# Two chunk loads of every expert joined into one 4 MB transfer, in a hybrid SSD/attention/MoE layer

## The chip, the cores and the metric

The kernel runs on one core of one Trainium2 chip. The metric is the device time of one execution in microseconds, the median of several runs. The core has TensorE (PE; its weight loads are shown apart as PEld), VectorE (DVE), ScalarE (ACT), GpSimd (POOL) and SyncE (SP), which here issues nearly all the transfers. 16 DMA engines move the data between HBM and SBUF.

## What is computed

One layer for 320 tokens (256 of a prompt, 64 of a sample): an SSD mixer and a band attention share one input projection and one output projection, and then comes a mixture of 32 experts, of which each token uses four. The change lies in the loads of the experts' weights.

```python
D_MODEL = 1024; N_EXPERTS = 32; TOP_K = 4; D_FF = 1024

xp = xp + merge_heads(y_ssm, o, att_norm_g[l], w_out[l])
xp = xp + moe_ffn(rms_norm(xp, norm_ffn_g[l]), w_router[l], b_router[l],
                  w_gate_up[l], b_gate_up[l], w_down[l], b_down[l])
...
def expert_block(args):
    xb, e = args
    gu = xb @ w_gate_up[e] + b_gate_up[e]          # (rows, 1024) @ (1024, 2048)
    gate = jnp.minimum(gu[:, :D_FF], SWIGLU_LIMIT)
    up = jnp.clip(gu[:, D_FF:], -SWIGLU_LIMIT, SWIGLU_LIMIT)
    act = (up + 1) * gate * jax.nn.sigmoid(gate * SWIGLU_ALPHA)
    return act @ w_down[e] + b_down[e]             # (rows, 1024) @ (1024, 1024)
```

All weights are float32. `w_gate_up[e]` has 8 MB and `w_down[e]` 4 MB, so 32 experts are 403 million bytes.

## The kernel before

**The ring.** `ring` is an SBUF tensor of six slots of 16 KB per partition, 2 MB each. The front of the kernel (input and output projection, attention, router) streams its weights through slots 0 to 4 (`FRONT_SLOTS`). After it, an expert's weights take all six slots, as six chunks: chunks 0 to 3 are quarters of `w_gate_up[e]` (`GU_CHUNKS`), chunks 4 and 5 halves of `w_down[e]` (`DN_CHUNKS`). `EXPERT_SLOT = (1, 2, 3, 4, 0, 5)` says which slot a chunk takes; slots 1 and 2 of chunks 0 and 1 are neighbours. The ring holds one expert and no more, so a chunk of the next expert is loaded as soon as PE has made its last use of the same chunk of this one.

**The rows.** Partition p of half h of an expert's matrix holds four successive rows of `w_gate_up[e]`, 32 KB in a piece. Chunk 0 takes the first two of the four for h = 0, chunk 1 the other two; chunks 2 and 3 do the same for h = 1. Chunk 3 is loaded as two transfers of 1 MB (L335, L336), of which the second counts on the semaphore `half_full`. All other chunks are one transfer of 2 MB with rows of 16 KB (L294, the helper `load`).

**SP, the queue of the loads.** SP issues in program order. Before the experts it loads chunk 0 of expert 0 once the last use of slot 1 in the front is over, chunk 1 once that of slot 2 is over (`wait_used`), then waits for three semaphores and issues four transfers of the attention's relative bias (L349, semaphore `bias_in`), and then the other chunks of expert 0. The loop `Fori(1, NE)` at L354 then loads expert n of the order: for each chunk it waits until the chunk is used (`used`: `gs_used` for chunk 0, `gs_used1` for chunk 1, `gs_used2`, `gu_mm`, `ds_used`, `d_mm`) and issues.

**PE, the user.** Tokens of an expert are worked on in blocks of up to 64 (`CAP`). `expert_pass(b, n)` is one block: for each gate/up chunk a wait for its slot's semaphore `w_full` and 16 matmuls (two 8-matmul rows of k), with `gather(b + 1)` before chunk 2; then `combine(b - 1)`, turning and placing; then chunks 4 and 5 at L2040, with `bias_products(b + 1)` between them. Most experts have one block. Four have two in this data (36 blocks in all); the weights stay in the ring for the second, and the semaphores of the first block are waited for by nobody, since SP waits for the count `first`, that of the expert's last block.

**DVE in the front.** DVE waits for `bias_in` at L1005 before it masks a corner of the bias (L1006), and after that it does `add_ssd(1)`, an addition of a part of the output projection (L979). PE waits for that addition (`out_ev`) before its first attention scores (L1695).

Of the kernel before, what the change touches and what calls it, by code (L numbers as in the profile page):

```python
# [34 lines left out]
FRONT_SLOTS = 5  # L35
# [7 lines left out]
N_IN, N_OUT = len(W_IN_CHUNKS), 3  # L43
FRONT = N_IN + N_OUT
GU_CHUNKS, DN_CHUNKS = 4, 2
EXPERT_SLOT = (1, 2, 3, 4, 0, 5)
# [13 lines left out]
def build(nc, x_prompt, x_sample, cache_k, cache_v, state_conv, state_ssm,  # L60
# [11 lines left out]
    with ctx:  # L72
        def sb(name, shape, dt=f32):
            return ctx.enter_context(nc.sbuf_tensor(name, shape, dt))

        def sem(name):
            return ctx.enter_context(nc.semaphore(name))


        ring = sb("ring", [128, SLOTS, SLOT])  # L80
# [185 lines left out]
        s = {n: sem(n) for n in names}  # L266
# [3 lines left out]
        w_full = [sem(f"w_full{i}") for i in range(SLOTS)]  # L270
# [8 lines left out]
        def slot_of(chunk):  # L279
            return chunk % FRONT_SLOTS  # L280
# [5 lines left out]
        def expert_arrival(c):  # L286

            return 16 * (len(range(EXPERT_SLOT[c], FRONT, FRONT_SLOTS)) if EXPERT_SLOT[c] < FRONT_SLOTS else 0) + 16


        @block.sync
        def _(sp):
            def load(slot, k, src):
                sp.dma_start(ring[:, slot, :].rearrange("p (k n) -> p k n", k=k), src).then_inc(w_full[slot], 16)  # L294

            def wait_used(i):

                if i < 3:
                    sp.wait_ge(s["proj_mm"], 4 * i + 4)
                elif i < 5:  # L300
                    sp.wait_ge(s["proj_mm"], 12 + NT * (i - 2))
                elif i < N_IN:
                    sp.wait_ge(s["lane_mm"], (LANE_Q, LANE_K, LANE_V)[i - 5])
                elif i < N_IN + 2:
                    sp.wait_ge(s["out_mm"], SSD_PARTS)
                else:
                    sp.wait_ge(s["out_mm"], OUT_PARTS)

            for t in range(2):
                sp.dma_start(x[:, t, :], x_prompt[0, 128 * t:128 * t + 128, :]).then_inc(x_in[t], 16)  # L310
            sp.dma_start(x[0:SS, 2, :], x_sample[0, :, :]).then_inc(x_in[2], 16)
            w3 = w_in[0].rearrange("(k p) n -> p k n", p=128)
            for i, c in enumerate(W_IN_CHUNKS):
                if i >= FRONT_SLOTS:
                    wait_used(i - FRONT_SLOTS)
                if i == 0:
                    slot = ring[:, 0, :].rearrange("p (k n) -> p k n", k=KD)
                    sp.dma_start(slot[:, 0:4, :], w3[:, 0:4, c:c + 512]).then_inc(half_full, 16)
                    sp.dma_start(slot[:, 4:8, :], w3[:, 4:8, c:c + 512]).then_inc(w_full[0], 16)
                else:  # L320
                    load(slot_of(i), KD, w3[:, :, c:c + 512])
            wo = w_out[0].rearrange("(k p) n -> p k n", p=128)
            for j in range(N_OUT):
                wait_used(N_IN + j - FRONT_SLOTS)
                load(slot_of(N_IN + j), 4, wo[:, 4 * j:4 * j + 4, :])

            def load_expert(e, c):
                if c < GU_CHUNKS:
                    w, h, k0, k = w_gate_up[0], c // 2, 2 * (c % 2), 2
                else:  # L330
                    w, h, k0, k = w_down[0], c - GU_CHUNKS, 0, 4
                rows = w[bass.ds(e, 1)].rearrange("a (h p k) n -> p (a h) k n", h=2, p=128)
                if c == GU_CHUNKS - 1:
                    slot = ring[:, EXPERT_SLOT[c], :].rearrange("p (k n) -> p k n", k=k)
                    sp.dma_start(slot[:, 0:1, :], rows[:, h, k0:k0 + 1, :]).then_inc(w_full[EXPERT_SLOT[c]], 16)  # L335
                    sp.dma_start(slot[:, 1:2, :], rows[:, h, k0 + 1:k0 + 2, :]).then_inc(half_full, 16)  # L336
                else:
                    load(EXPERT_SLOT[c], k, rows[:, h, k0:k0 + k, :])

            for c in range(GU_CHUNKS + DN_CHUNKS):  # L340
                slot = EXPERT_SLOT[c]
                wait_used(max(range(slot, FRONT, FRONT_SLOTS)) if slot < FRONT_SLOTS else N_IN)
                load_expert(0, c)
                if c == 1:
                    sp.wait_ge(s["ext_out"], 17)
                    sp.wait_ge(s["seg_mm"], 6)
                    sp.wait_ge(s["y_mm"], 5)
                    for q in range(4):
                        sp.dma_start(bias[:, 2 * q:2 * q + 2, :], bass.AP(  # L349
                            table_d, head_of(q // 2, 2 * (q % 2)) * 383, [[1, 128], [2 * 383, 2], [1, 256]]))\  # L350
                            .then_inc(s["bias_in"], 16)
            sp.wait_ge(s["order_ready"], 1)
            used = ["gs_used", "gs_used1", "gs_used2", "gu_mm", "ds_used", "d_mm"]
            with sp.Fori(1, NE) as n:  # L354
                e = sp.value_load(order[0:1, bass.ds(n, 1)], min_val=0, max_val=NE - 1)
                first = sp.value_load(before[0:1, bass.ds(n, 1)], min_val=1, max_val=MAX_BLOCKS)
                for c in range(GU_CHUNKS + DN_CHUNKS):

                    sp.wait_ge(s[used[c]], first)
                    load_expert(e, c)  # L360

            for t in range(2):
                sp.wait_ge(s["fin_ready"], t + 1)
                sp.dma_start(y_prompt[0, 128 * t:128 * t + 128, :], xn[:, t, :]).then_inc(s["y_out"], 16)
            sp.wait_ge(s["fin_ready"], 3)
            sp.dma_start(y_sample[0, :, 0:HALF], xn[0:SS, 2, 0:HALF]).then_inc(s["y_out"], 16)
            sp.wait_ge(s["y_out"], 4 * 16)
            sp.wait_ge(s["vt_out"], NT * 16)
            sp.wait_ge(s["kt_out"], NT * 16)
            sp.wait_ge(s["cso_out"], 2 * 16)  # L370
            sp.wait_ge(s["sout_out"], 2 * 16)
# [999 lines left out]
        def _(pe):  # L1371
# [31 lines left out]
            n = [0]  # L1403
# [79 lines left out]
            for t in range(NT):  # L1483
                rows = ROWS[t]
# [32 lines left out]
            for t in range(NT):  # L1517
                rows, hc = ROWS[t], slice(HCOL[t], HCOL[t] + ROWS[t])
# [458 lines left out]
            def expert_pass(b, n, beside=None):  # L1977

                pe.wait_ge(s["xt_ev"], b + 1)
                for c in range(GU_CHUNKS):  # L1980
# [3 lines left out]
                        places(0)  # L1984
                    if not beside and c == 2:
                        gather(b + 1)
                    pe.wait_ge(w_full[EXPERT_SLOT[c]], expert_arrival(c) + 16 * n)
                    w = ring[:, EXPERT_SLOT[c], :].rearrange("p (k n) -> p k n", k=2)

                    def gate_up(kk, m):  # L1990
# [60 lines left out]
            turn(0)  # L2051
            idle_products(7, 2)
            expert_pass(0, 0, beside=True)
            pe.wait_ge(s["zeros_ready"], 1)
            total = pe.value_load(blocks[0:1, 0:1], min_val=NE, max_val=MAX_BLOCKS)
# [5 lines left out]
def head_of(group, n):  # L2061

    return 4 * group + 2 * (n % 2) + n // 2
# [89 lines left out]
```

## Time and profile before

| | |
|---|---|
| median of 3 runs | 1272.1 us |
| lowest, highest | 1271.05, 1275.47 us |
| profiled execution | 1272.46 us, with a span of 1270.7 us in the trace |
| PE busy | 1232.4 us, 97% of the span |
| DVE, ACT, POOL busy | 38%, 17%, 3% |
| DMA | 436.6 MB, 344 GB/s over the span |
| granted PE clock | 1.0 but for a few us |

The page cuts the span into 40 slices of 31.8 us. From the tenth slice on (286 us) the experts run. There PE is busy throughout, and the DMA engines move 427 to 429 GB/s in all slices but those in which an expert has its second block: 259, 333, 303 and 292 GB/s. So two resources are nearly full at once, and what counts is which of the two is waited for, and where.

Times in the text are from the start of the span. "Expert 0" is the first in the order, and an expert's start is the start of its first matmul at L1993.

### The profile page before, as it was taken

The page shows a single profiled execution, that of the slowest core. Times are in us where ns is not written, and L with a number is a line of the kernel's source. Part 1 is how long each engine was busy: PE and PEld are TensorE (multiplying, and loading weights), DVE is VectorE, ACT ScalarE, POOL GpSimd, SP SyncE. Part 2 cuts the span into 40 slices and gives each one's busy share as a digit, 9 for nine tenths or more (in the row PEclk, how much of TensorE's full clock was granted, in tenths as well). Part 3 has the DMA queues.
Part 4 walks back from the last instruction along what each step waited for, and adds up shares of the span by engine and source line. Part 5 has one row for each costly group of instructions (what it writes and reads, how often), then busy time and mean ns, then how long its engine had stood idle before and what let it go on. Part 6 is the DMA issues. An engine that isn't in the chain of part 4 may idle for free.

```text
span 1270.7 us, 17573 instructions
## 1 busy us (share of the span) xinstructions
PE 1232.4 (97%) x6386; PEld 553.0 (44%) x6387; DVE 480.8 (38%) x1038; ACT 215.2 (17%) x444; POOL 39.0 (3%) x67
## 2 busy tenths in 40 slices
PE   9999999999999999999999999989999999999996
PEld 7656754653334443434333434333434333334332
DVE  3743545466532332324322224222234232234234
ACT  1032223562201111011001111010111110111102
POOL 2000002401000000000000000000000000000000
PEclk9999999999999999999999999999999999999999
DMA  9631234328999969999998999997999999799995
GB/s 329 219 133 68 83 132 137 130 109 341 428 428 427 427 259 429 429 428 426 428 386 333 429 427 429 427 427 303 417 427 427 428 429 426 292 429 428 427 427 239
DMA packets 48202, 436.60 MB, mean 344 GB/s; under 512 B 6293, under 2 KB 7437, under 8 KB 19510
## 3 DMA queue, kind: packets, MB, share of 16 engines
q1 hardware_dynamic: 44000, 429.28, 81.2%
q0 software_dynamic: 2176, 6.74, 1.6%
q10 hardware_dynamic: 2006, 0.31, 0.2%
q8 instruction: 13, 0.21, 0.1%
q14 instruction: 7, 0.06, 0.0%
HBM read 432.59 MB, written 3.72 MB: 343 GB/s over the span
## 4 chain that ended last, share of the span: by engine, by line
PE 83%; DMA 13%; DVE 2%; issue 1%; ACT 0%; DVEq 0%; SPq 0%; ACTq 0%
PE PS L1993 33%; PE PS L2040 17%; DMA ring<-in_w_gate_up_dram 12%; PE PS L1422 6%; PE PS L1431 5%; PE PS L1886 4%; PE PS L1376 4%; PE PS L1917 3%; PE PS L1911 2%; PE PS L1433 1%; PE PS L1465 1%; PE PS L1755 1%; PE PS L1974 1%; PE PS L1729 1%; PE PS L1613 1%
## 5 line engine op out<-in xcount | busy, mean ns | idle before, releaser
L1993 PE MATMUL PS<-ring,r 128*64 128x512 f32 x2304 | 510.7, 593 | 16.1 <-DMA ring<-in_w_gate_up_dram 15.7
L1993 PEld LDWEIGHTS PS<-ring,r 128*64 128x64 f32 x2304 | 167.5, 137 | 331.8 <-issue 289.2
L2040 PE MATMUL PS<-ring,r 128*64 128x512 f32 x1152 | 261.5, 595 | 4.5 <-ACT r L778 0.5
L1318 DVE TENSOR_SCALAR r<-PS 128x256 f32<-128x256 f32 x72 | 27.2, 419 | 333.2 <-PE PS L1993 333.1
L2040 PEld LDWEIGHTS PS<-ring,r 128*64 128x64 f32 x1152 | 81.8, 137 | 135.6 <-issue 129.0
L1222 DVE SCALAR_TENSOR_TENSOR r<-PS,gprev,r 128x512 f32<-128x512 f32 x185 | 127.9, 743 | 0.6 <-PE PS L1917 0.6
L1346 DVE TENSOR_TENSOR yy<-PS,yy 128x512 fp32r<-128x512 f32 x36 | 24.9, 691 | 193.4 <-ACT yy L783 193.4
L1376 PE MATMUL PS<-ident,r 128*128 128x128 f32 (+4 forms) x491 | 70.3, 282 | 1.7 <-DMA r<-in_x_sample_dram 0.5
L1422 PE MATMUL PS<-r,ring 128*128 128x323 f32 x256 | 71.9, 436 | 0.0
L767 ACT ACTIVATE r<-PS 128x512 f32<-128x512 f32 x35 | 20.9, 597 | 295.4 <-PE PS L1886 295.4
L783 ACT ACTIVATE yy<-PS 128x512 fp32r<-128x512 f32 x36 | 21.5, 597 | 276.8 <-PE PS L2040 276.8
L1376 PEld LDWEIGHTS PS<-ident,r 128*128 128x128 f32 (+4 forms) x491 | 58.2, 181 | 20.9 <-DVE r L1328 8.9
L1422 PEld LDWEIGHTS PS<-r,ring 128*128 128x128 f32 x256 | 48.1, 189 | 22.5 <-issue 1.9
L771 ACT ACTIVATE r<-r 128x256 f32<-128x256 f32 x72 | 26.9, 416 | 183.3 <-DVE r L1318 183.3
L1886 PE MATMUL PS<-r,pm 128*64 128x512 bf16 x420 | 51.4, 379 | 1.4 <-DVE pm L1195 1.4
L1917 PE MATMUL PS<-yy,place 64*128 64x512 f32 x296 | 44.5, 418 | 0.8 <-ACT yy L783 0.8
L1431 PE MATMUL PS<-ring,r 128*128 128x512 f32 x96 | 42.1, 593 | 0.0
L1886 PEld LDWEIGHTS PS<-r,pm 128*64 128x64 bf16 x420 | 25.2, 110 | 35.7 <-issue 20.1
L1917 PEld LDWEIGHTS PS<-yy,place 64*128 64x128 f32 x296 | 24.9, 184 | 34.4 <-issue 30.8
L1190 DVE COPY pcur<-pg 128x3 f32 x36 | 6.1, 169 | 79.2 <-issue 79.2
L774 ACT ACTIVATE place<-PS 128x384 fp32r<-128x384 f32 x36 | 17.7, 492 | 82.4 <-PE PS L1911 82.4
L1431 PE MATMUL PS<-ring 128*128 128x512 f32 x64 | 29.4, 603 | 2.2 <-DVE r L979 2.2
(349 smaller groups left out, 864.0 us busy)
## 6 DMA issues: line engine op xcount, KB each, us to landing
ring<-in_w_gate_up_dram SPq DMA_DIRECT2D x96, 2048.0 KB, 15.6
ring<-in_w_down_dram SPq DMA_DIRECT2D x64, 2048.0 KB, 16.2
ring<-in_w_gate_up_dram SPq DMA_DIRECT2D x64, 1024.0 KB, 16.2
ring<-in_w_in_dram SPq DMA_DIRECT2D x7, 2048.0 KB, 15.6
ring<-in_w_out_dram SPq DMA_DIRECT2D x3, 2048.0 KB, 7.5
ring<-in_w_in_dram SPq DMA_DIRECT2D x2, 1024.0 KB, 9.0
r<-in_x_prompt_dram SPq DMA_DIRECT2D x2, 512.0 KB, 4.1
r<-in_x_prompt_dram POOLq DMA_DIRECT2D x2, 512.0 KB, 4.8
```

Source lines behind the costliest of these rows:

```text
L771: a.activation(sg[:, part], ug[:, part], ACT.Sigmoid, scale=ALPHA).then_inc(s["sig_ready"], 1)
L1222: v.scalar_tensor_tensor(xx, bank(banks[i]), gprev[:, t:t + 1], xx, ALU.mult, ALU.add).then_inc(s["o_ev"], 1)
L1318: v.tensor_scalar(ug[:, part], bank(0)[:, part], LIMIT, None, ALU.min).then_inc(s["g_ready"], 1)
L1346: v.tensor_tensor(yy2[:, 1, :], bank(2), yy2[:, 0, :].bitcast(f32), ALU.subtract)\
L1376: return nc.tensor.transpose(out, in_, ident[0:k, 0:k])
L1422: last = mm(PS[:, b, 0:HC], w[:, k, 128 * m:128 * m + 128], hT[:, k, :], start=(k == 0), stop=(k == KD - 1))
L1431: return mm(PS[:, b, :], lhs, rhs, start=first, stop=end)
L1886: last = mm(PS[64 * h:64 * h + 64, 3, :], pm[:, t, 64 * h:64 * h + 64], xb[t][:, part, 512 * h:512 * h + 512], start=(t == 0 and part == 0 ...
L1911: last = mm(bank(banks[4]), place[:, 256:384], yy2[:, part, :], start=(part == 0), stop=(part == 1))
L1917: last = mm(bank(banks[2 * t + h]), place[half, 128 * t:128 * t + 128], yy2[half, part, :], start=(part == 0), stop=(part == 1))
L1993: last = mm(PS[64 * h:64 * h + 64, m, :], xt[:, k % 4, k // 4, :], w[:, kk, D * m + 512 * h:D * m + 512 * h + 512], start=False, stop=(k = ...
L2040: last = mm(PS[64 * h:64 * h + 64, 2, :], at[:, kk, c, :], w[:, kk, 512 * h:512 * h + 512], start=(c == 0 and kk == 0), stop=(c == 1 and k ...
```

## The change

Chunks 0 and 1 become one transfer of 4 MB, from rows of 32 KB to the 32 KB of slots 1 and 2 in each partition. It counts on the semaphore of slot 1. In the loop SP issues it after `gs_used1`, the last use of chunk 1; `gs_used` isn't waited for any more. PE waits for it before chunk 0, and no more before chunk 1. For expert 0 the transfer is issued once slot 1 and slot 2 are both free.

```diff
                 rows = w[bass.ds(e, 1)].rearrange("a (h p k) n -> p (a h) k n", h=2, p=128)
-                if c == GU_CHUNKS - 1:
+                if c == 0:
+                    pair = ring[:, EXPERT_SLOT[0]:EXPERT_SLOT[0] + 2, :].rearrange("p s (k n) -> p (s k) n", k=k)
+                    sp.dma_start(pair, rows[:, h, 0:4, :]).then_inc(w_full[EXPERT_SLOT[0]], 16)
+                elif c == GU_CHUNKS - 1:
...
             for c in range(GU_CHUNKS + DN_CHUNKS):
-                slot = EXPERT_SLOT[c]
-                wait_used(max(range(slot, FRONT, FRONT_SLOTS)) if slot < FRONT_SLOTS else N_IN)
+                if c == 1:
+                    continue
+                for slot in EXPERT_SLOT[0:2] if c == 0 else EXPERT_SLOT[c:c + 1]:
+                    wait_used(max(range(slot, FRONT, FRONT_SLOTS)) if slot < FRONT_SLOTS else N_IN)
                 load_expert(0, c)
-                if c == 1:
+                if c == 0:
                     sp.wait_ge(s["ext_out"], 17)
...
-            used = ["gs_used", "gs_used1", "gs_used2", "gu_mm", "ds_used", "d_mm"]
+            used = ["gs_used1", None, "gs_used2", "gu_mm", "ds_used", "d_mm"]
...
-                for c in range(GU_CHUNKS + DN_CHUNKS):
+                for c in (0, 2, 3, 4, 5):
...
-                    pe.wait_ge(w_full[EXPERT_SLOT[c]], expert_arrival(c) + 16 * n)
+                    if c != 1:
+                        pe.wait_ge(w_full[EXPERT_SLOT[c]], expert_arrival(c) + 16 * n)
```

SP's queue before the experts: the last load of the output projection, the first chunks of expert 0, the bias (`r<-bias_table_clipped`) and chunk 2. Before:

```order
L294 DMA ring<-in_w_out_dram 128x4x1024 [waits lane_mm]
L294 DMA ring<-in_w_gate_up_dram 128x4096 [waits lane_mm] x2
L349 DMA r<-bias_table_clipped 128x2x256 [waits y_mm,seg_mm,ext_out]
L349 DMA r<-bias_table_clipped 128x2x256 x3
L294 DMA ring<-in_w_gate_up_dram 128x4096 [waits out_mm]
```

and changed:

```order
L294 DMA ring<-in_w_out_dram 128x4x1024 [waits lane_mm]
L335 DMA ring<-in_w_gate_up_dram 128x8192 [waits lane_mm]
L354 DMA r<-bias_table_clipped 128x2x256 [waits y_mm,seg_mm,ext_out]
L354 DMA r<-bias_table_clipped 128x2x256 x3
L294 DMA ring<-in_w_gate_up_dram 128x4096 [waits out_mm]
```

Chunk 0 no longer goes out ahead of chunk 1 at its own wait; both stand right before the bias.

SP's queue in the loop over experts, one pass. Before:

```order
L294 ISA [waits gs_used]
L294 DMA ring<-in_w_gate_up_dram 128x4096
L294 ISA [waits gs_used1]
L294 DMA ring<-in_w_gate_up_dram 128x4096
L294 ISA [waits gs_used2]
L294 DMA ring<-in_w_gate_up_dram 128x4096
```

and changed:

```order
L335 ISA [waits gs_used1]
L335 DMA ring<-in_w_gate_up_dram 128x8192
L294 ISA [waits gs_used2]
L294 DMA ring<-in_w_gate_up_dram 128x4096
L338 ISA [waits gu_mm]
L338 DMA ring<-in_w_gate_up_dram 128x2048
```

What stood behind `gs_used` now stands behind `gs_used1`; all the rest keeps its place.

PE at the first block, chunks 0 and 1 of expert 0 (in the loop the same waits stand against a register). Before:

```order
L1993 MATMUL PS<-ring,r 64x512 [waits w_full1,xt_ev]
L1993 MATMUL PS<-ring,r 64x512
L1966 MATMUL PS<-spare,ones 128x66 [waits turns_ready]
L1993 MATMUL PS<-ring,r 64x512 x6
L1993 MATMUL PS<-ring,r 64x512 [waits w_full2]
L1993 MATMUL PS<-ring,r 64x512 x7
```

and changed:

```order
L1999 MATMUL PS<-ring,r 64x512 [waits w_full1,xt_ev]
L1999 MATMUL PS<-ring,r 64x512
L1971 MATMUL PS<-spare,ones 128x66 [waits turns_ready]
L1999 MATMUL PS<-ring,r 64x512 x14
L1381 MATMUL PS<-ident,bej 1x128 [waits bej_ready]
```

The wait for slot 2 in the middle is gone; the one for slot 1 now stands for both.

## Rows read from the trace of the kernel before

**Rows 1.** The page: PE's busy time, and the gate/up matmuls (idle before, by releaser)

```profile
PE 1232.4 (97%) x6386; PEld 553.0 (44%) x6387; DVE 480.8 (38%) x1038; ACT 215.2 (17%) x444; POOL 39.0 (3%) x67
...
L1993 PE MATMUL PS<-ring,r 128*64 128x512 f32 x2304 | 510.7, 593 | 16.1 <-DMA ring<-in_w_gate_up_dram 15.7
```

**Rows 2.** Busy time by stretch: engines, granted clock, DMA share, GB/s

```profile
504.70:609.70 105.00, 104.54 (x556) 41.78 (x552) 34.63 (x76) 12.13 (x24) 0.00 (x0) 1.00 1.01 428
611.30:640.70 29.40, 26.69 (x138) 9.96 (x138) 8.68 (x20) 3.03 (x6) 0.00 (x0) 1.00 1.01 428
```

**Rows 3.** PE's timeline (start, duration, idle before): blocks' first matmuls, and waits

```profile
426.54 7.04 PE L1993 MATMUL PS<-ring,r 128*64 128x512 f32 x32
...
452.72 7.04 PE L1993 MATMUL PS<-ring,r 128*64 128x512 f32 x32
...
611.26 3.65 PE L1993 MATMUL PS<-ring,r 128*64 128x512 f32 x16 [1.17 <-DMA ring<-in_w_gate_up_dram]
616.15 3.65 PE L1993 MATMUL PS<-ring,r 128*64 128x512 f32 x16 [1.24 <-DMA ring<-in_w_gate_up_dram]
...
640.73 3.65 PE L1993 MATMUL PS<-ring,r 128*64 128x512 f32 x16 [1.17 <-DMA ring<-in_w_gate_up_dram]
...
655.49 2.80 PE L1993 MATMUL PS<-ring,r 128*64 128x512 f32 x12 [0.20 <-DMA ring<-in_w_gate_up_dram]
668.83 7.04 PE L1993 MATMUL PS<-ring,r 128*64 128x512 f32 x32
...
885.00 7.04 PE L1993 MATMUL PS<-ring,r 128*64 128x512 f32 x32
...
1101.08 7.04 PE L1993 MATMUL PS<-ring,r 128*64 128x512 f32 x32
...
1231.97 7.04 PE L1993 MATMUL PS<-ring,r 128*64 128x512 f32 x32
```

**Rows 4.** SP's timeline (start, duration): issues of chunks 0 and 1

```profile
327.49 0.33 SPq L294 DMA_DIRECT2D ring<-in_w_gate_up_dram  x1
...
456.51 0.34 SPq L294 DMA_DIRECT2D ring<-in_w_gate_up_dram  x1
...
459.94 0.33 SPq L294 DMA_DIRECT2D ring<-in_w_gate_up_dram  x1
...
1108.30 0.33 SPq L294 DMA_DIRECT2D ring<-in_w_gate_up_dram  x1
```

**Rows 5.** Timelines of SP, DVE and PE (in this order) around the bias

```profile
183.99 0.34 SPq L294 DMA_DIRECT2D ring<-in_w_gate_up_dram  x1
...
188.77 2.59 SPq L349 DMA_DIRECT2D r<-bias_table_clipped  x4
...
198.39 0.48 DVE L1006 MEMSET r<- 64x512 f32 x1 [4.37 <-DMA r<-bias_table_clipped]
198.91 0.75 DVE L979 SCALAR_TENSOR_TENSOR r<-PS,stat,r 128x512 f32<-128x512 f32 x1
...
201.07 0.68 DVE L1012 TENSOR_TENSOR r<-r,PS 64x512 f32<-64x512 f32 x1 [0.82 <-PE PS L1616]
...
211.21 0.75 DVE L979 SCALAR_TENSOR_TENSOR r<-PS,stat,r 128x512 f32<-128x512 f32 x1 [3.73 <-PE PS L1431]
...
200.80 0.71 PE L1695 MATMUL PS<-r 64*128 64x128 f32 x8
...
207.47 3.70 PE L1431 MATMUL PS<-ring 128*128 128x512 f32 x8 [0.79 <-DVE r L979]
```

**Rows 6.** Busy time by stretch, while chunk 3 of an expert is transferred

```profile
650.10:655.00 4.90, 4.90 (x30) 1.67 (x24) 0.00 (x0) 0.60 (x1) 0.00 (x0) 1.00 1.04 433
```

**Rows 7.** The chain: the same eight matmuls, twice

```profile
251.08 3.65 PE PS L1755 x8
...
258.28 5.29 PE PS L1755 x8
```

**Rows 8.** Busy time by stretch: the granted clock (0.54) in the second of these

```profile
258.00:260.00 2.00, 2.00 (x5) 0.98 (x5) 1.33 (x4) 1.99 (x8) 0.00 (x0) 0.54 0.00 0
```

## The prediction

> **What bounds the kernel now.** First the page. PE is busy 97% of the span, and the gate/up matmuls waited only 15.7 us for their weights [rows 1], so PE looks like the bound. Then the busy time by stretch: while experts with one block follow each other, the DMA engines are full too, at 428 GB/s [rows 2]. So the third view decides, PE's timeline. A block of an expert whose weights are there takes PE 26.18 us, from 426.54 to 452.72 [rows 3]. An expert's 12.58 million bytes need more: where PE waits for them, the period is 640.73 - 611.26 = 29.47 us [rows 3], which is 427 GB/s, or **4.912 us for each 2 MB chunk**. PE gains 3.29 us per expert on the transfers. What lets it run at its own pace in between is a cushion. While an expert has its second block, nothing is loaded until the ring is released, and afterwards the next expert lies there well before it is wanted. Every single expert then eats 3.29 us of that lead. Second blocks begin at 452.72, 668.83, 885.00 and 1101.08, eight blocks apart, which at PE's own pace would be 209.4 us and is 216.1 to 216.2: three stretches of 6.7 us lost each, in the two experts before every next second block (611.26 and 640.73 for the first stretch). Before 452.72 and after 1101.08 no block is late [rows 3]. The waits come in three small pieces, 1.17 and 1.24 us at chunks 0 and 1, 0.20 us within chunk 3 [rows 3]. So what bounds the kernel is PE for most of the experts, and the transfers for the last two of each stretch; how many these are is set by the cushion. What a change of the loads does to the time is what it does to the cushion.
>
> **The cushion after the change.** I call the expert whose second block starts at 452.72 expert 5, the next ones 6 to 12; expert 12 is the next with two blocks (starts 640.73 and 668.83). Two things shorten the lead. The pair is issued at the last use of chunk 1 instead of chunk 0: 459.94 instead of 456.51, 3.43 us later [rows 4]. And PE may start an expert only when 4 MB of it have landed, where before it could start with 2 MB and was held last by chunk 3. The sum for this stretch: before, the second half of chunk 3 of expert 12 let PE go on at 655.49 [rows 3]. It was chunk-length 40 of those issued from 456.51 on (six experts of 6, and 4), 40 x 4.912 = 196.47, which leaves 2.51 us of fixed delay. The changed order issues from 459.94 on, and expert 12 can start after 38 chunk-lengths (six experts of 6, and the pair): 459.94 + 186.65 + 2.51 = 649.1. Its first block then takes 26.18 us unhindered (chunk 2 lands 4.9 us after the start and is wanted after 8.6; the rest has as much slack), and its second block starts at 675.3 instead of 668.83: **6.4 us later**. Three such stretches (the periods 216.17 and 216.08 say they are alike) make **19.3 us**.
>
> The same rule makes the two outer parts late, which weren't. Up to expert 5: the pair of expert 2 is issued at 327.49, where chunk 1 was [rows 4]; the pair of expert 5 is there after three experts of 6 and 2, 20 chunk-lengths: 327.49 + 98.24 + 2.51 = 428.2 against a start at 426.54 [rows 3]: **1.7 us**. After the last second block: pair issue at 1108.30 [rows 4], the pair of the last expert is there after 26 chunk-lengths, 1108.30 + 127.71 + 2.51 = 1238.5, against 1231.97 [rows 3]: **6.5 us**. Together 1.7 + 19.3 + 6.5 = **27.5 us**. None of it can be won back, since each stretch starts anew from a full ring. That the queue doesn't run dry, which would cost more: the pair of expert 7 is issued when expert 6 has used its chunk 1, by PE's pace at 452.72 + 26.18 + 7.2 = 486.1, while the transfers of expert 6 last till 459.94 + about 2 + 29.5 = 491.4. Later in the stretch, the pair is ready to go some 12 us ahead.
>
> **The front.** One more place comes before the experts. SP issues chunk 1 of expert 0 at 183.99 and the bias at 188.77, in that order on one queue [rows 5]. Chunk 0 had gone long before. Now the pair of 4 MB is issued at 183.99, and the bias stands behind 2 MB more: 4.9 us. DVE already waited 4.37 us for the bias, until 198.39, and so did the addition at 198.91 to 199.66 behind it [rows 5]; PE needs that addition for its scores at 200.80 [rows 5], so there is a slack of 1.1 us. Moved by 4.9 us, the addition ends at 204.6 and PE's scores start 3.8 us late. Behind them DVE has only an idle 0.82 us to give (before 201.07), so its chain is 4.1 us late, and PE's L1431 at 207.47 waits for that chain [rows 5]. From there on DVE waits for PE (3.73 us before 211.21), so PE leads and the delay stays: **4.1 us**. The nearest bounds: other queues' traffic shares the engines at that time and would share the pair instead of the bias, so 3.5 to 5.3 us for the bias, 2.5 to 4.5 us for the end. I take the 4.1 of the plain chunk length.
>
> **What is removed.** PE's wait before chunk 1 and one transfer per expert; SP is idle nearly all the time and its issue of 0.33 us hides. That leaves the rate of longer rows. The only rows of another length in the experts are the 8 KB of chunk 3, which moved at 433 GB/s in one stretch [rows 6], no slower than 16 KB at 428 [rows 2]; so length isn't what holds the rate. I take no gain. If the pairs alone went at 433 (4.84 us per chunk-length), 8, 3 x 14 and 10 of them on the three kinds of stretches save 0.07 us each, 4.2 us.
>
> The Trainium skill (DMA: Bandwidth & Descriptors, "Anatomy of one DMA" and "Rules for kernel authors") gives one transfer about 2 us fixed plus its bytes at 436 GB/s, and advises to join small transfers into a large one. By that, an expert's seven queued transfers would take 14 us beyond their bytes, and one fewer would save 2 us each time; the 29.47 us for 12.58 million bytes [rows 3] leave room for at most 0.6 us in all, so the trace doesn't agree for transfers that are queued. The 2.51 us above, paid once per stretch, is the place of that fixed part.
>
> **The sum.** 1272.46 us of the profiled execution (0.4 us above the median, and 1.8 above its own span) + 27.5 + 4.1 = 1304.1 us.
>
> **The rivals.**
> - *The clock falls.* Now all of an expert's waiting stands in one piece of up to 3.3 us (29.47 - 26.18), at four experts of each long stretch and two of the last. In the trace of before, eight matmuls that take 3.65 us took 5.29 at a granted clock of 0.54, half speed (1.2 of 2.4 GHz), after a stretch of small matmuls [rows 7, 8]: 1.64 us. Against it: with the waits in pieces of 1.24 us at most, the clock held. Where an expert waits after it anyway, the loss is hidden; it counts at the last expert of a stretch and in the front, five places: up to 8.2 us, 1312. One or two of them lie within my range. The Trainium skill (TensorE: Matmul & The Clock Gate, "HAM oscillation") describes waits for weights after which each tile starts at the slow clock; no stretch of this trace shows a wait as long as the one expected here.
> - *The front absorbs the bias.* If POOL's traffic moves out of the bias's way and gives back most of the 4.9 us, 1300.
> - *Long rows stream a little faster*: by the 4.2 us above, 1300.
> - *The wait only moves.* If the lead were long enough for both demands, only the front would be left: 1276.6. Against it stands that PE runs out of data at 611 already before the change [rows 3].
> - *Faster than before.* 32 KB rows would have to lift the transfers so far that the lead outlives a stretch. Expert 12's second block keeps its 668.83 if the 14 chunk-lengths in pairs take 62.3 instead of 68.8 us, 471 GB/s; that is the point from which it decides. At 500 GB/s a pair takes 8.4 us, each of the three stretches ends 3.6 us early, the outer parts even: 1272.5 - 10.8 + 2.7 = 1264. No stretch of the trace moves more than 433 [rows 6].
>
> **How the numbers follow.** The forecast, with no or one or two falls of the clock, 0.74; the clock falling nearly everywhere 0.08; the front absorbed 0.06; rows faster by a little 0.06; only the front 0.02; faster than before 0.03; the rest 0.01. The predicted time is 1304. The range takes in both milder cases and half of the clock's: 1298 to 1310. A measurement of this kernel can tell about 0.3% (3.8 us) from no change. Slower 0.95, same 0.02, faster 0.03.
>
> **What the profile would show.** The gate/up matmuls' wait for their weights up from 15.7 to about 45 us, nearly all before chunk 0 and in pieces of about 3.3 us, in experts 9 to 12, 16 to 19, 23 to 26 and the last two, with 1 to 2 us at expert 5; distances between second blocks of 222.6 us instead of 216.1; the pair landing as one; still 427 GB/s in full stretches; DVE's wait for the bias at 9 us instead of 4.37 and a gap in PE of about 4 us at 201; PE's busy time unchanged but for the clock. Wrong would be: distances still at 216 (the lead suffices), or below (faster rows), or above 225 (a queue run dry, a slow clock), and no gap in the front.

## The result, and the profile after

The changed kernel takes 1310.07 us (median of 3 runs, 1309.82 to 1310.24) against 1272.1 us: 1.0296 of the time before, 95% interval 1.0282 to 1.0310. That is 38 us slower, on the side and by the mechanism forecast, 6 us above the 1304 and at the very edge of the range of 1298 to 1310. The profiled execution took 1309.82 us with a span of 1308.1 us, 37.4 us more than the span before. Two disturbed executions are left out of the ratios and medians below: one of the sixth kernel's four (3259 us) and one of the kernel before beside it (1816 us).

The page of the changed kernel, in the order of its parts: busy time, the slices' transfer rate, the queues, and the groups of the gate/up matmuls.

```profile
PE 1246.0 (95%) x6386; PEld 555.8 (42%) x6387; DVE 481.9 (37%) x1038; ACT 215.3 (16%) x444; POOL 39.1 (3%) x67
...
GB/s 328 204 129 66 81 135 126 106 139 302 428 431 426 405 197 430 429 430 428 432 348 291 429 428 435 424 430 257 383 434 428 424 428 426 217 433 422 427 427 207
DMA packets 43595, 436.60 MB, mean 334 GB/s; under 512 B 5782, under 2 KB 6926, under 8 KB 18999
...
L1999 PE MATMUL PS<-ring,r 128*64 128x512 f32 x2304 | 521.5, 606 | 33.5 <-DMA ring<-in_w_gate_up_dram 33.1
```

PE's wait for the gate/up weights rose from 15.7 us [rows 1] to 33.1 us, and the same 2304 matmuls are busy 10.8 us longer. The forecast was a wait of 45 us in pieces of 3.3; part of that lateness shows as slow matmuls instead, and 33.1 + 10.8 = 43.9 us is near it. The rate of a full slice is about what it was (424 to 435 GB/s). The mean fell from 344 to 334 GB/s because the pauses of the transfers, at the second blocks, grew. The packets tell that the 4 MB transfer really goes out as rows of 32 KB: 4607 fewer than before.

PE's timeline of the changed kernel, from expert 0 to the second block of expert 12, as start, duration and idle time before (expert 5 starts at 438.67, its second block at 466.59, expert 12 at 662.33, its second block at 688.56):

```profile
296.58 1.08 PE L1999 MATMUL PS<-ring,r 128*64 128x512 f32 x4 [0.41 <-DVE r L1218]
...
409.28 7.09 PE L1999 MATMUL PS<-ring,r 128*64 128x512 f32 x32 [1.40 <-DMA ring<-in_w_gate_up_dram]
...
438.67 8.78 PE L1999 MATMUL PS<-ring,r 128*64 128x512 f32 x32 [2.98 <-DMA ring<-in_w_gate_up_dram]
...
466.59 7.04 PE L1999 MATMUL PS<-ring,r 128*64 128x512 f32 x32
...
574.20 8.78 PE L1999 MATMUL PS<-ring,r 128*64 128x512 f32 x32 [2.69 <-DMA ring<-in_w_gate_up_dram]
...
603.58 7.09 PE L1999 MATMUL PS<-ring,r 128*64 128x512 f32 x32 [1.27 <-DMA ring<-in_w_gate_up_dram]
...
632.95 8.78 PE L1999 MATMUL PS<-ring,r 128*64 128x512 f32 x32 [2.97 <-DMA ring<-in_w_gate_up_dram]
...
662.33 7.09 PE L1999 MATMUL PS<-ring,r 128*64 128x512 f32 x32 [1.29 <-DMA ring<-in_w_gate_up_dram]
...
688.56 7.04 PE L1999 MATMUL PS<-ring,r 128*64 128x512 f32 x32
...
910.46 7.04 PE L1999 MATMUL PS<-ring,r 128*64 128x512 f32 x32
...
1132.47 7.04 PE L1999 MATMUL PS<-ring,r 128*64 128x512 f32 x32
...
1269.47 7.09 PE L1999 MATMUL PS<-ring,r 128*64 128x512 f32 x32 [1.27 <-DMA ring<-in_w_gate_up_dram]
```

Where before each late expert waited in three pieces [rows 3], all waiting stands before chunk 0. It begins at expert 9 in this stretch, where before it began at expert 11. The distances between second blocks, which answer to [rows 3], are 221.97, 221.90 and 222.01 us instead of 216.1 to 216.2. The two kinds of rows also differ: after a wait of 2.7 us or more the 32 matmuls take 8.78 us, after 1.3 us they take 7.09. The busy time by stretch tells why; the column before the last two is the granted clock:

```profile
574.20:577.60 3.40, 3.40 (x12) 1.21 (x14) 0.85 (x4) 0.00 (x0) 0.00 (x0) 0.70 1.05 448
603.60:607.00 3.40, 3.40 (x16) 1.18 (x18) 0.92 (x5) 0.00 (x0) 0.00 (x0) 1.00 1.04 443
633.00:636.40 3.40, 3.40 (x10) 1.02 (x12) 0.85 (x4) 0.00 (x0) 0.00 (x0) 0.58 1.03 439
```

And the front, which answers to [rows 5]: SP's, DVE's and PE's timelines.

```profile
184.26 0.34 SPq L335 DMA_DIRECT2D ring<-in_w_gate_up_dram  x1
188.96 2.10 SPq L354 DMA_DIRECT2D r<-bias_table_clipped  x4
...
206.39 0.48 DVE L1011 MEMSET r<- 64x512 f32 x1 [12.16 <-DMA r<-bias_table_clipped]
206.91 0.75 DVE L984 SCALAR_TENSOR_TENSOR r<-PS,stat,r 128x512 f32<-128x512 f32 x1
...
207.81 1.23 PE L1700 MATMUL PS<-r 64*128 64x128 f32 x8 [6.63 <-DVE r L984]
208.97 6.05 PE L1436 MATMUL PS<-ring 128*128 128x512 f32 x8
...
216.47 3.70 PE L1436 MATMUL PS<-ring 128*128 128x512 f32 x8
```

DVE waits 12.16 us for the bias instead of 4.37, PE has a gap of 6.63 us, and right behind it eight matmuls take 6.05 us that take 3.70 later; the mean granted clock from 208.9 to 215.0 us was 0.60.

The 37.4 us of the span, by place:

| place | forecast | before | after | measured |
|---|---|---|---|---|
| start to expert 0 | +4.1 | 289.25 | 296.58 | +7.3 |
| expert 0 to second block of expert 5 | +1.7 | 163.47 | 170.01 | +6.5 |
| three distances between second blocks | +19.3 | 648.36 | 665.88 | +17.5 |
| fourth second block to last expert | +6.5 | 130.89 | 137.00 | +6.1 |
| last expert to the end | 0 | 38.73 | 38.63 | -0.1 |

(289.25 is the first matmul of expert 0 before the change, by its PE timeline.)

### The profile page after: what moved, and what is told of

It reads as the page before. It is cut to its first block, busy times and chain, and to the rows that moved or that the text cites. A ratio compares the mean times of both kernels' runs of the same rounds, so it can differ in the third digit from the quotient of the medians.

```text
span 1308.1 us, 17480 instructions
## 1 busy us (share of the span) xinstructions
PE 1246.0 (95%) x6386; PEld 555.8 (42%) x6387; DVE 481.9 (37%) x1038; ACT 215.3 (16%) x444; POOL 39.1 (3%) x67
## 2 busy tenths in 40 slices
DMA packets 43595, 436.60 MB, mean 334 GB/s; under 512 B 5782, under 2 KB 6926, under 8 KB 18999
## 4 chain that ended last, share of the span: by engine, by line
PE 69%; DMA 26%; DVE 2%; issue 2%; ACT 0%; DVEq 0%; SPq 0%; ACTq 0%
PE PS L1999 30%; DMA ring<-in_w_gate_up_dram 26%; PE PS L2046 11%; PE PS L1427 5%; PE PS L1436 5%; PE PS L1381 3%; PE PS L1891 3%; PE PS L1922 2%; PE PS L1438 1%; PE PS L1470 1%; PE PS L1760 1%; PE PS L1916 1%; PE PS L1734 1%; PE PS L1979 1%; PE PS L1618 1%
## 5 line engine op out<-in xcount | busy, mean ns | idle before, releaser
L1999 PE MATMUL PS<-ring,r 128*64 128x512 f32 x2304 | 521.5, 606 | 33.5 <-DMA ring<-in_w_gate_up_dram 33.1
L2046 PE MATMUL PS<-ring,r 128*64 128x512 f32 x1152 | 261.5, 595 | 4.5 <-ACT r L783 0.5
L1351 DVE TENSOR_TENSOR yy<-PS,yy 128x512 fp32r<-128x512 f32 x36 | 24.9, 692 | 193.4 <-ACT yy L788 193.4
## 6 DMA issues: line engine op xcount, KB each, us to landing
ring<-in_w_down_dram SPq DMA_DIRECT2D x64, 2048.0 KB, 19.3
```

The costliest lines, as they stand in the source:

```text
L1351: v.tensor_tensor(yy2[:, 1, :], bank(2), yy2[:, 0, :].bitcast(f32), ALU.subtract)\
L1999: last = mm(PS[64 * h:64 * h + 64, m, :], xt[:, k % 4, k // 4, :], w[:, kk, D * m + 512 * h:D * m + 512 * h + 512], start=False, stop=(k = ...
L2046: last = mm(PS[64 * h:64 * h + 64, 2, :], at[:, kk, c, :], w[:, kk, 512 * h:512 * h + 512], start=(c == 0 and kk == 0), stop=(c == 1 and k ...
```

## The experiments

The theory is the forecast's: an expert's weights are wanted with a lead that the ring gives after each second block; the change takes 3.4 us of it by issuing later and about 3 by starting later; and the bias behind 4 MB instead of 2 is a separate loss in the front. The rivals: only one of the two halves matters; the long transfer itself costs or gains; the front's loss has another cause. All times of the kernel before beside these runs lie between 1271.7 and 1272.4 us in the median.

**One half each.** The first kernel only issues later:

```diff
-            used = ["gs_used", "gs_used1", "gs_used2", "gu_mm", "ds_used", "d_mm"]
+            used = ["gs_used1", "gs_used1", "gs_used2", "gu_mm", "ds_used", "d_mm"]
```

> Two transfers as before; only in the loop SP issues chunk 0 after the last use of chunk 1 (3.43 us later), PE's waits and the front stay. Cushion theory: each stretch between second blocks loads 3.4 us later, so the three long stretches and the last each lose 3.4, the first about 0.6: 1272.1 + 14 = 1286 (1284 to 1289), distances between second blocks 219.5 us. Rival, that the later issue hides behind the queue and only PE's later start costs: 1272, distances of 216.1.

Measured: 1286.9 us (1286.04 to 1288.3) against 1272.4, ratio 1.011 (1.0094 to 1.0127). PE's timeline, first matmuls of three of the second blocks (the durations are cut at the edge of the stretch asked for) and the last expert before the second of them:

```profile
455.66 1.89 PE L1993 MATMUL PS<-ring,r 128*64 128x512 f32 x8
...
646.83 3.65 PE L1993 MATMUL PS<-ring,r 128*64 128x512 f32 x16 [1.15 <-DMA ring<-in_w_gate_up_dram]
651.73 3.65 PE L1993 MATMUL PS<-ring,r 128*64 128x512 f32 x16 [1.25 <-DMA ring<-in_w_gate_up_dram]
...
661.59 2.79 PE L1993 MATMUL PS<-ring,r 128*64 128x512 f32 x12 [0.19 <-DMA ring<-in_w_gate_up_dram]
...
674.94 5.33 PE L1993 MATMUL PS<-ring,r 128*64 128x512 f32 x24
...
894.36 6.18 PE L1993 MATMUL PS<-ring,r 128*64 128x512 f32 x28
```

The first two distances are 219.3 and 219.4 us, 3.3 above those before. The rival (nothing lost) is out. The waits stay in three small pieces, and no matmul behind them is slow. The total fits the forecast partly by luck: from expert 0 to the second block of expert 5 it is 2.4 us more than before (0.6 was forecast), from the fourth second block to the last expert 1.4 more (3.4 was forecast).

The second kernel only starts later, PE waiting for both chunks:

```diff
+                    if c == 0:
+                        pe.wait_ge(w_full[EXPERT_SLOT[1]], expert_arrival(1) + 16 * n)
                     pe.wait_ge(w_full[EXPERT_SLOT[c]], expert_arrival(c) + 16 * n)
```

> Two transfers issued as before; only PE waits for chunk 1 as well before it starts chunk 0. Cushion theory: what held PE before was the second half of chunk 3, which let an expert start when about 1.4 chunk-lengths had landed; now it is 2, some 3 us more in each of the three long stretches and the last, nothing in the first: 1272.1 + 12 = 1284 (1282 to 1287), distances of 219 us, waits of 3.3 us in one piece before chunk 0. Rival, that only the issue matters: 1272.

Measured: 1291.64 us (1287.53 to 1293.1), ratio 1.0145 (1.0121 to 1.0168). Both halves cost, then, but this one more than forecast. The profiled execution has distances of 220.9, 219.3 and 221.0 us. The last expert before the next second block, in the first and the second of these:

```profile
648.31 8.68 PE L1995 MATMUL PS<-ring,r 128*64 128x512 f32 x32 [3.04 <-DMA ring<-in_w_gate_up_dram]
...
869.21 7.09 PE L1995 MATMUL PS<-ring,r 128*64 128x512 f32 x32 [1.59 <-DMA ring<-in_w_gate_up_dram]
```

Where that expert's matmuls run at full clock the distance is the 219 forecast; where they run slow it is 1.6 us more. So 3.2 us of the 7.6 over the forecast are the clock. Another 1.7 are in the part up to the second block of expert 5, forecast at nothing: expert 5 already waits 1.5 us. The rest is spread: the slow-free distance is 3.2 and not 3 us longer, from the fourth second block to the last expert it takes 134.3 us (1116.42 to 1250.68) instead of 130.9, where 3 were forecast, and this execution reached expert 0 at 290.06 us instead of 289.25.

**Both halves, as two transfers and as one.** The third kernel has both edits above and still moves 2 MB at a time in rows of 16 KB. The fourth has the change itself, but only in the loop:

```diff
-                if c == GU_CHUNKS - 1:
+                if c == 0 and joined:
+                    pair = ring[:, EXPERT_SLOT[0]:EXPERT_SLOT[0] + 2, :].rearrange("p s (k n) -> p (s k) n", k=k)
+                    sp.dma_start(pair, rows[:, h, 0:4, :]).then_inc(w_full[EXPERT_SLOT[0]], 16)
+                elif c == GU_CHUNKS - 1:
...
-            used = ["gs_used", "gs_used1", "gs_used2", "gu_mm", "ds_used", "d_mm"]
+            used = ["gs_used1", None, "gs_used2", "gu_mm", "ds_used", "d_mm"]
...
-                for c in range(GU_CHUNKS + DN_CHUNKS):
+                for c in (0, 2, 3, 4, 5):
                     sp.wait_ge(s[used[c]], first)
-                    load_expert(e, c)
+                    load_expert(e, c, joined=True)
...
-                    pe.wait_ge(w_full[EXPERT_SLOT[c]], expert_arrival(c) + 16 * n)
+                    if c != 1 or beside:
+                        pe.wait_ge(w_full[EXPERT_SLOT[c]], expert_arrival(c) + 16 * n)
```

> Both at once in the loop, still as two transfers of 2 MB with rows of 16 KB, front as before. Cushion theory: the whole loss of the loop without the front, and without any gain of long rows: 1272.1 + 31 to 34 = 1303 to 1306 (distances 222 to 223 us, the clock's fall at some waits included). Rival, that the transfer of 4 MB itself (its length, its rows) costs: clearly below the loop-only kernel of this call.

> The 4 MB transfer in the loop alone; expert 0 is loaded as before (chunk 0 early, chunk 1 ahead of the bias). The changed kernel's trace puts 7.3 us of its loss before the experts and 30.1 after: 1310.1 - 7.3 = 1302.8 (1301 to 1304), with no gap of PE near 201 us. If 32 KB rows save 0.1 us per pair, it is up to 3 us below the kernel with two transfers; if they do nothing, equal. Rival, that the late bias isn't the cause of the front's loss: 1310.

Measured: 1302.87 us (1302.11 to 1303.35) with two transfers, ratio 1.0237 (1.0220 to 1.0254), and 1302.35 us (1301.12 to 1306.77) with one, ratio 1.0241 (1.0217 to 1.0265). They can't be told apart. So the size of the transfer and the length of its rows are worth nothing that shows in the time; the loss in the loop is that of the two waits. In the timelines a small gain is there. Starts of two late experts in a row, first of the kernel with two transfers, then with one:

```profile
593.63 7.09 PE L1995 MATMUL PS<-ring,r 128*64 128x512 f32 x32 [1.34 <-DMA ring<-in_w_gate_up_dram]
623.09 8.68 PE L1995 MATMUL PS<-ring,r 128*64 128x512 f32 x32 [3.05 <-DMA ring<-in_w_gate_up_dram]
```

```profile
595.21 8.59 PE L1996 MATMUL PS<-ring,r 128*64 128x512 f32 x32 [2.98 <-DMA ring<-in_w_gate_up_dram]
624.58 7.09 PE L1996 MATMUL PS<-ring,r 128*64 128x512 f32 x32 [1.47 <-DMA ring<-in_w_gate_up_dram]
```

29.46 us per expert against 29.37: 0.09 us for each joined pair. Over all late experts in a row the means are 29.45 (10 periods) and 29.38 us (11 periods), 0.07 us apart. Whether the longer rows give that or the one transfer fewer was not separated.

**The front alone.** The fifth kernel has the 4 MB transfer for expert 0 only, the sixth holds chunk 0 of expert 0 back to the time of chunk 1 and sends both as two transfers of 2 MB. The edit of the sixth:

```diff
             for c in range(GU_CHUNKS + DN_CHUNKS):
-                slot = EXPERT_SLOT[c]
-                wait_used(max(range(slot, FRONT, FRONT_SLOTS)) if slot < FRONT_SLOTS else N_IN)
+                for slot in EXPERT_SLOT[0:2] if c < 2 else EXPERT_SLOT[c:c + 1]:
+                    wait_used(max(range(slot, FRONT, FRONT_SLOTS)) if slot < FRONT_SLOTS else N_IN)
                 load_expert(0, c)
```

> The 4 MB transfer for expert 0 alone; the loop over the other experts as before. If the front's loss stands by itself: DVE's wait for the bias near 12 us instead of 4.4, a gap of PE of about 6.6 us after 201 us with the clock at half behind it, the first expert 7.3 us later, 1272.4 + 7.5 = 1280 (1278.5 to 1281.5). Rival, that the 7 us are partly taken back in the experts' cushion: 1275 or less.

> Only the front: chunk 0 of expert 0 is held back to the time of chunk 1, and both go as two transfers of 2 MB with rows of 16 KB right behind each other, ahead of the bias. If the bias is late by the bytes ahead of it and by the other queue's loads that now fall on it: as with the one transfer, 1280, DVE's wait for the bias 11.5 to 12.5 us. Rival, that packets of 32 KB hold the other queue's packets of 4 KB back and so push them onto the bias: DVE's wait 9 to 10.5 us, 1276 to 1278.

Measured: 1280.99 us (1280.65 to 1281.02), ratio 1.0073 (1.0055 to 1.0091), and 1281.86 us (1279.79 to 1282.31), ratio 1.0074 (1.0053 to 1.0096). DVE's wait for the bias, of the one and of the other:

```profile
206.17 0.48 DVE L1011 MEMSET r<- 64x512 f32 x1 [12.21 <-DMA r<-bias_table_clipped]
```

```profile
209.12 0.48 DVE L1006 MEMSET r<- 64x512 f32 x1 [12.20 <-DMA r<-bias_table_clipped]
```

The wait is the same to 0.01 us (the sixth kernel's front as a whole ran 3 us later in this execution), so rows of 32 KB aren't what holds the bias back. Bytes are. The transfers of the kernel before from 184 to 198 us, when the bias was in, and of the changed one from 184 to 206 us (q1 is SP's queue, q0 GpSimd's; packets and MB):

```profile
q1 hardware_dynamic: 1232, 3.15, 70.5%
q0 software_dynamic: 321, 1.05, 24.3%
```

```profile
q1 hardware_dynamic: 1232, 5.24, 64.5%
q0 software_dynamic: 640, 2.10, 25.6%
```

The pair's 4.2 MB keep the engines longer, and GpSimd's transfers are held up with the bias and then move beside it. The trace's packets tell the two apart. Before, the last packet of chunk 1 ended at 191.46 us, and the bias's own packets (1024 of 1 KB) ran from 192.43 to 197.95, with 0.46 MB of GpSimd's within that time. In the changed kernel the pair ended at 197.30, and the bias ran from 196.93 to 205.89, with 1.79 MB of GpSimd's within it. So of the 8.0 us by which the bias came later (206.39 against 198.39) 4.5 are the later start, near the 4.9 forecast, and 3.4 the slower transfer of the bias itself, 8.96 us instead of 5.52.

The seventh kernel is the changed one with the bias issued ahead of expert 0's pair, the eighth the one before with the bias ahead of chunk 1. For both the edit is one of place: the call `load_expert(0, c)` stands behind the block that waits for `ext_out`, `seg_mm` and `y_mm` and issues the bias, not ahead of it.

> The changed kernel, with the bias issued ahead of expert 0's pair. If the front's loss is the order on SP's queue: no gap of PE at 201 us, DVE's wait for the bias under 4 us, 1310.1 - 7.7 = 1302.4 (1301 to 1304.5). Rival, that the pair now comes late for expert 0 or delays later loads of the front: 1305 or more. Rival, that the bias isn't the cause: 1310.

> The kernel before, with the bias issued ahead of chunk 1 of expert 0 instead of behind it. DVE's wait of 4.4 us should shrink to under 1.5 us, and yet the time stay, since the chain behind the bias is released by PE's matmuls at 201 us as well: 1272.4 (1271 to 1273.5). Rival, that the wait for the bias is on the path: 1270 or less.

Measured: 1300.19 us (1299.28 to 1302.38), ratio 1.0227 (1.0208 to 1.0245), and 1272.13 us (1270.71 to 1273.61) against 1271.97, ratio 1.0004 (0.9994 to 1.0013). The seventh takes away 9.9 us of the change's 38, somewhat more than the 7.7 forecast, and PE has no gap:

```profile
198.04 0.48 DVE L1011 MEMSET r<- 64x512 f32 x1 [3.63 <-DMA r<-bias_table_clipped]
...
201.19 0.71 PE L1700 MATMUL PS<-r 64*128 64x128 f32 x8
```

That order is therefore the cause of the front's loss. One expectation failed: DVE's wait didn't go under 1.5 us in the kernel before. With the bias ahead of chunk 1 it is 3.91 us there, 3.63 in the changed kernel. The bias is then issued at 188.8 us, after the three semaphores, and its packets still run from 190.66 to 197.50, hardly earlier than the 197.95 of the kernel before. GpSimd's transfers and the load behind the bias move in the same time; what each of them costs it wasn't tried. In the kernel before nothing is to be gained from the order, as expected: PE leads there.

**Why expert 5 is late.** The tenth kernel is the loop-only one, with GpSimd's three loads of the last norm's gain held back:

```diff
             pool.wait_ge(s["gates_held"], 1)
+            pool.wait_ge(s["d_mm"], 6)
```

> The loop-only kernel, with GpSimd's three loads of the last norm's gain (768 KB) held back until the sixth block's end, when the transfers pause. If these loads on expert 1's transfers are what made expert 5 late by 3 us more than the sum said: from the first matmul of expert 0 to the second block of expert 5 165 to 168.5 us instead of 170.5 (before: 163.5), 1302.4 - 3 = 1299.5 (1298 to 1301.5). Rival, that they don't matter: 170.5 us, 1302.4.

Measured: 1301.97 us (1299.46 to 1304.56), ratio 1.0230 (1.0212 to 1.0248); the total doesn't tell it from 1302.35 and missed the 1298 to 1301.5 expected. The timelines do. Expert 0, expert 5 and its second block, of the loop-only kernel and of this one:

```profile
287.83 1.08 PE L1996 MATMUL PS<-ring,r 128*64 128x512 f32 x4 [0.41 <-DVE r L1215]
...
430.35 8.78 PE L1996 MATMUL PS<-ring,r 128*64 128x512 f32 x32 [2.97 <-DMA ring<-in_w_gate_up_dram]
...
458.28 1.03 PE L1996 MATMUL PS<-ring,r 128*64 128x512 f32 x4
```

```profile
288.03 1.08 PE L1997 MATMUL PS<-ring,r 128*64 128x512 f32 x4 [0.41 <-DVE r L1216]
...
428.12 8.78 PE L1997 MATMUL PS<-ring,r 128*64 128x512 f32 x32 [2.60 <-DMA ring<-in_w_gate_up_dram]
...
456.05 7.04 PE L1997 MATMUL PS<-ring,r 128*64 128x512 f32 x32
```

Expert 5 starts 140.1 us after expert 0 instead of 142.5, and expert 4 has no wait any more. From expert 0 to the second block of expert 5 it is 168.0 us, within the expectation, where the loop-only kernel, the changed one and the seventh all have 170.0 to 170.5. So 2.4 us of this part's 6.5 are those loads, which fell on the transfers of expert 1. Further on this execution lost more than that to the clock: its expert 12 took 10.02 us for 32 matmuls and its expert 19 8.59, and the first two distances are 224.7 and 223.3 us instead of 221.9 and 221.8.

**The other way round.** If less lead costs, more should pay. The ninth kernel loads chunk 0 in two halves of 1 MB and issues the first half after 8 of its 16 matmuls (semaphores for the halves added, bias ahead of chunk 1 as in the eighth):

```diff
+                if c == 0 and halves is not None:
+                    slot = ring[:, EXPERT_SLOT[c], :].rearrange("p (k n) -> p k n", k=k)
+                    sp.dma_start(slot[:, 0:1, :], rows[:, h, k0:k0 + 1, :]).then_inc(s["gain_in"], 16)
+                    sp.wait_ge(s["gs_used"], halves * 2 + 1)
+                    sp.dma_start(slot[:, 1:2, :], rows[:, h, k0 + 1:k0 + 2, :]).then_inc(w_full[EXPERT_SLOT[c]], 16)
```

> The other way round: chunk 0 of every expert in two transfers of 1 MB, the first issued after 8 of the chunk's 16 matmuls, bias ahead of expert 0's chunk 1, all else as before. Cushion theory: after a second block the transfers start 1.7 us earlier, of which the later releases (chunk 2 is used 12 us after the start) leave 0.7 us per long stretch: 1272.0 - 2 = 1270 (1269 to 1271), distances between second blocks 215.4 instead of 216.1 us. Rival, that one more transfer per expert costs its fixed part: 1272 or more.

Measured: 1278.5 us (1278.08 to 1281.67) against 1271.73, ratio 1.0057 (1.0043 to 1.0071): 7 us slower, where 2 us faster were expected. The distances are 217.9, 218.6 and 218.4 us. PE's timeline at the last expert before two of the second blocks, and the granted clock behind the first wait:

```profile
644.97 5.35 PE L2002 MATMUL PS<-ring,r 128*64 128x512 f32 x16 [2.70 <-DMA ring<-in_w_gate_up_dram]
...
1081.94 5.35 PE L2002 MATMUL PS<-ring,r 128*64 128x512 f32 x16 [2.69 <-DMA ring<-in_w_gate_up_dram]
```

```profile
645.00:648.40 3.40, 3.40 (x10) 1.13 (x12) 0.00 (x0) 0.00 (x0) 0.00 (x0) 0.57 1.00 424
```

Chunk 0 is no longer waited for, and what was 1.17 and 1.24 us at chunks 0 and 1 [rows 3] is one wait of 2.7 us at chunk 1. Behind it 16 matmuls take 5.35 us instead of 3.65, in two of the three stretches at the expert that counts, in the other at the one before (835.32). From the end of that wait to the second block it is then 24.5 us instead of 23.2, so the clock accounts for 2.6 us of the 6.5 by which the three distances grew. The other 3.9 are chunk 1 of the last expert, which comes later and not earlier: 193.4, 195.4 and 193.9 us after the preceding second block, where before it was 192.9 to 193.0 in all three. The earlier issue does give a lead, and loses it at once. From 2 to 12 us behind a second block the transfers now have 341 to 346 GB/s instead of 288, but from 12 to 30 us 401 to 406 instead of 426 to 427. First of the kernel before, then of this one, at the first of the second blocks:

```profile
464.72:482.72 18.00, 17.89 (x94) 7.30 (x92) 7.76 (x15) 2.43 (x5) 0.00 (x0) 1.00 1.01 427
```

```profile
463.57:481.57 18.00, 17.89 (x94) 7.30 (x92) 7.76 (x15) 2.44 (x5) 0.00 (x0) 1.00 1.00 401
```

By 30 us the lead is down to some 0.1 to 0.2 MB, less than half a microsecond of transfer. Why the rate is lower there, and where the rest goes, wasn't tried. So the reverse of the change does not show that more lead pays: this experiment leaves that open.

## Why the prediction was right, and what it missed

- **What bounds.** Right: the time is set by the lead of the transfers, stretch by stretch, and the change costs lead. The experts that wait (9 to 12 and so on, and the last two) and the distances are as told; the size of the single waits is not: 2.7 to 3.0 us and 1.3 by turns, where 3.3 each were forecast.
- **The three stretches, 19.3 us.** Measured 17.5. Distances of 222.0 where 222.6 were forecast: the period of a late expert is 29.38 us (662.33 - 632.95) and not 29.47, and the seven pairs from the issue for expert 6 to the start of expert 12 make 0.6 us of that, the difference. I had taken no gain and named 433 GB/s as the bound; the true gain is a tenth of a microsecond per expert. The halves add up in these stretches, too: late issue 3.3 us per stretch, late start 3.2 us without the clock.
- **The last part, 6.5 us.** Measured 6.1. Here the halves alone cost less, 1.4 and 3.4 us, since each alone first uses up the slack of about 1.8 us that the forecast's own sum leaves the last expert (3.4 + 4.9 - 6.5).
- **Up to expert 5, 1.7 us.** Measured 6.5, the worst term. The step that failed is the one that took the pair of expert 2 to start on idle engines at its issue (327.49) and added 2.51 us. The engines were still busy with expert 1, whose transfers had started late and shared the engines with GpSimd's loads; those alone are 2.4 us. Another 1.7 us is the clock, which fell behind expert 5's wait (8.78 us instead of 7.04), at an expert whose lateness counts.
- **The front, 4.1 us.** The step was right in kind and mis-sized: the bias came 8.0 us late and not 4.9. The 2 MB more on SP's queue cost what the sum said, nearly: the bias's packets start 4.5 us later. The step that failed is the one that let GpSimd's traffic share the pair instead of the bias, with a bound of 5.3 us for which no working is given. That traffic fell on the bias, 1.79 MB instead of 0.46, and made its transfer 3.4 us longer. With the fall of the clock behind the gap (2.4 us more for eight matmuls) the front costs 9.0 us by the front-only kernel and 9.9 by taking it out; the profiled executions show 7.3, since that of before had a fall of its own at 258 us [rows 7], 1.6 us, that the other had not.
- **The clock.** One or two falls were in the forecast, falls nearly everywhere had 0.08. It fell at 8 of the 16 late experts, and then cost nothing in most, since the next expert's wait shrank from 3 to 1.3 us. It cost 1.7 us at expert 5 and 2.4 in the front. The rows fit a pattern of every other one: a slow expert ends late, and no fall follows the short wait after it. With four late experts in a stretch and the first one hit, the last is spared; the forecast had no reason for that, so that the total stayed at the edge of the range is in part luck. In other executions the fall meets the last expert of a stretch, as in the second kernel above. The Trainium skill (TensorE: Matmul & The Clock Gate, "HAM oscillation") describes waits for the next slice of data after which a tile starts at the slow clock, and these rows agree: of the 54 single waits for the pair of 2.49 to 3.08 us in the six kernels that have them (the changed one, the second, third, fourth, seventh and tenth), 41 were followed by a slow expert; of those of 1.24 to 1.85 us none was. The trace of the kernel before did hold one PE wait as long as those expected, though not for weights: 4.09 us for ScalarE, before 1265.38 us near the end, and the mean granted clock went from 1.00 (1262 to 1264) over 0.78 to 0.50 (1266 to 1268). It could have given the rival more than 0.08.
- **Rows of 32 KB.** The Trainium skill's advice to join small transfers (DMA: Bandwidth & Descriptors, "Rules for kernel authors") would, by the fixed cost of about 2 us that the page gives for one transfer, save that for each pair. That figure is the page's fit for transfers that GpSimd issues; these are issued by SP. The trace disagrees for transfers that are queued behind one another: 0.07 to 0.09 us.
- **A side sum.** The rival "faster than before" adds 2.7 us to 1272.5 - 10.8 without saying from what; with the prediction's own 4.1 us for the front it is 1265.8 and not 1264. Nothing in the forecast rests on it.

## What to carry to other kernels

With a ring that holds one unit of work, count for each piece when it is released and when it is wanted, not how many transfers there are; joining two pieces takes the later release of the two and the later arrival, and pays for both in every stretch in which the transfers have to catch up. When a transfer is moved ahead of another on one queue, count the bytes that then go first and also what other queues will move beside the one that is held back. And where PE must wait, several waits of a microsecond were better here than one of three.

## What the runs showed of the hardware that was not expected

- A source row of 32 KB that is contiguous on both sides goes out as one packet: 4607 packets fewer, of which 4096 are the 32 joined transfers of 128 rows and 511 are under 512 B (6293 before, 5782 after). The joined transfer gains 0.07 to 0.09 us per 4 MB, under 1% of the pair's 9.8 us. There is no sign that long packets hold back GpSimd's packets of 4 KB or the bias's of 1 KB: DVE's wait for the bias was as long with rows of 16 KB.
- The granted clock had a mean of 0.55 to 0.70 in the stretches of 3.4 us read just behind single waits of 2.7 to 3.0 us of PE (in part of each it was the lower level, 1.2 GHz), and 1.00 behind a wait of 1.3 us. By the time of the 32 matmuls behind it, a single wait of 2.49 to 3.08 us was followed by a fall in 41 cases of 54. Three waits of 1.1 to 1.3 and 0.2 us within one expert, of nearly the same sum, were followed by none in the first kernel. Which of the long waits are hit differs between executions; the second kernel's runs spread over 5.6 us (1287.53 to 1293.1).
- Issuing a chunk in two halves, the first one earlier, made the transfers start 1.7 us sooner and run at 401 to 406 GB/s for the next 18 us instead of 427, so that nearly all of the head start was gone 30 us later.
